# Turning the gated activations in an expert stage: three of four products with the identity become transposes

## What is computed

```python
a = jnp.einsum('nd,edf->nef', t, w_gate)
u = jnp.einsum('nd,edf->nef', t, w_up)
act = jax.nn.silu(a) * u * gate[..., None].astype(h.dtype)
out = jnp.einsum('nef,efd->nd', act, w_down)
```

## Time and profile before

| | us |
|---|---|
| median of 3 runs | 1609.87 |
| lowest and highest run | 1607.52, 1611.09 |
| the profiled execution | 1609.71 |
| its span, first to last instruction | 1608.0 |
| TensorE busy in the span | 1483.1 |
| DVE, ACT, POOL busy | 583.6, 175.2, 657.1 |

### The profile page before, as it was taken

The page is one execution under the profiler, slowest core; times in us unless marked ns, Lnnn a source line. Parts: engine busy times, 40 slices in busy tenths (PEclk is TensorE's granted clock), DMA queues, the critical chain, the costliest instruction groups (busy, mean ns, idle before and its releaser), DMA issues.

```text
span 1608.0 us, 24420 instructions
## 1 busy us (share of the span) xinstructions
PE 1483.1 (92%) x9906; PEld 1154.6 (72%) x9906; DVE 583.6 (36%) x1042; ACT 175.2 (11%) x281; POOL 657.1 (41%) x498
## 2 busy tenths in 40 slices
PE   5789999999959979999999899869999999999996
PEld 3789999998859969988777699754554454545534
DVE  3927668749561241112111621241212112212204
ACT  3000221000000000012222100121000000000002
POOL 4557697879947737753444557200000000000000
PEclk9889999999979989999999999979999999999998
DMA  7234444445534434463888434808999999999971
GB/s 236 79 118 145 130 158 131 157 157 186 174 104 147 153 105 150 146 259 128 325 327 330 146 132 157 340 1 354 397 422 399 396 423 397 379 423 397 400 311 59
DMA packets 106097, 376.99 MB, mean 234 GB/s; under 512 B 12405, under 2 KB 12405, under 8 KB 76274
## 3 DMA queue, kind: packets, MB, share of 16 engines
q1 hardware_dynamic: 103762, 371.68, 61.3%
q10 hardware_dynamic: 2272, 4.42, 0.8%
HBM read 369.30 MB, written 6.77 MB: 234 GB/s over the span
## 4 chain that ended last, share of the span: by engine, by line
PE 85%; DVE 11%; ACT 2%; issue 1%; DMA 1%; DVEq 0%; ACTq 0%; SPq 0%
PE ps L752 36%; PE ps L1048 14%; PE ps L799 11%; PE ps L1096 7%; PE ps L1110 4%; PE ps L1026 4%; PE ps L856 2%; DVE hT L1471 2%; DVE hT L1643 1%; PE ps L1065 1%; PE ps L874 1%; PE ps L864 1%; DVE hT L1420 1%; DMA A<-in_x_sample 1%; PE ps L695 1%
## 5 line engine op out<-in xcount | busy, mean ns | idle before, releaser
L752 PE MATMUL ps<-hT,tiles 128*128 128x144 f32 x2816 | 470.7, 291 | 49.3 <-ACT kv_stage L1234 16.8
L752 PEld LDWEIGHTS ps<-hT,tiles 128*128 128x128 f32 x2816 | 401.6, 194 | 52.8 <-issue 23.8
L652 POOL TENSOR_TENSOR tiles<-tiles 128x512 f32<-128x512 f32 x88 | 123.4, 1402 | 228.8 <-DMA tiles<-in_w_in 89.8
L1048 PE MATMUL ps<-tiles,A 128*64 128x512 f32 x576 | 171.2, 601 | 1.3 <-DVE A L1876 1.3
L752 PE MATMUL ps<-tiles 128*128 128x144 f32 x960 | 172.1, 289 | 0.0
L1441 DVE COPY pair_sums<-ps 128x144 f32<-128x144 f32 x44 | 13.5, 308 | 354.6 <-PE ps L752 354.6
L752 PEld LDWEIGHTS ps<-tiles 128*128 128x128 f32 x960 | 141.3, 193 | 0.0
L752 PE MATMUL ps<-A,tiles 128*128 128x144 f32 x768 | 138.2, 289 | 0.0
L799 PE MATMUL ps<-tiles,mT 128*128 128x256 f32 x512 | 133.3, 383 | 4.1 <-ACT kv_stage L1234 4.1
L655 POOL TENSOR_TENSOR tiles<-tiles 128x512 f32<-128x512 f32 x88 | 122.8, 1396 | 0.0
L657 POOL TENSOR_TENSOR tiles<-tiles 128x512 f32<-128x512 f32 x88 | 118.3, 1344 | 6.9
(11 more groups left out here) (287 smaller groups left out, 1741.6 us busy)
## 6 DMA issues: line engine op xcount, KB each, us to landing
tiles<-in_expert_w_down SPq DMA_DIRECT2D x56, 1024.0 KB, 10.0
tiles<-in_w_in SPq DMA_DIRECT2D x40, 1024.0 KB, 5.1
tiles<-in_expert_w_gate SPq DMA_DIRECT2D x40, 1024.0 KB, 11.3
A<-in_expert_w_up SPq DMA_DIRECT2D x32, 1024.0 KB, 9.4
tiles<-in_expert_w_up SPq DMA_DIRECT2D x32, 1024.0 KB, 12.6
tiles<-in_xa_w_k SPq DMA_DIRECT2D x16, 1024.0 KB, 5.1
tiles<-in_w_out SPq DMA_DIRECT2D x16, 1024.0 KB, 5.0
tiles<-in_xa_w_q SPq DMA_DIRECT2D x16, 1024.0 KB, 5.1
```

What stands on the lines that cost most here:

```text
L652: step.tick(tt(s1, a21, a22, ALU.add))
L752: return mm(one(u + mp, x, TH), w[:, kp, mp, :], rhs, start=(first and g == 0 and kp == 0), stop=(g == 3 and kp == 1), skip_group_check=True)
L1048: m = mm(ps[C * n:C * n + C, BRANCH_BANK, :], xe[:, b, C * s:C * s + C], moe_tile(t + 2 * g + n).rearrange("p (k n) -> p k n", k=KT)[:, k, :],
```

## The change

The four turns of `turn_act` were four matmuls with the identity. Now the first block is still such a matmul, and the other three are transposes with the same operands, the same identity and the same places in PSUM. The signal stays on the last one. `turn_act` is called twice a pair.

```diff
@@ -1062,8 +1062,11 @@
             def turn_act():
 
                 for k in range(KT):
-                    m = mm(ps[:, ACT_BANK, k * C:(k + 1) * C], act_nat[0:C, k * P:(k + 1) * P], ident[0:C, 0:C],
-                           start=True, stop=True)
+                    dst, own = ps[:, ACT_BANK, k * C:(k + 1) * C], act_nat[0:C, k * P:(k + 1) * P]
+                    if k == 0:
+                        mm(dst, own, ident[0:C, 0:C], start=True, stop=True)
+                    else:
+                        m = nc.tensor.transpose(dst, own, ident[0:C, 0:C])
                 m.then_inc(unit_done, 1)
```

## The result

| | before | after |
|---|---|---|
| median of 7 runs, us | 1607.79 | 1600.38 |
| lowest and highest, us | 1604.80, 1613.58 | 1593.77, 1601.44 |
| span of the profiled execution, us | 1608.0 | 1598.5 |

A forecast was written before the change was run, and what follows sets the result against it. TensorE was taken to bound the kernel. Turns of 0.52 us for 1.03 save 0.51 each, 16 x 0.51 = 8.1 us, bringing the median from 1609.87 to 1601.8 us; range 1599.2 to 1605.4.

The forecast's parts named there:

- The bound: Expert stage: TensorE sets the pace, the transfers have 2.6 us a pair in hand, so cuts in TensorE's stream shorten it.
- The passes: Each of 16 turns: three transposes replace six product passes, 0.52 us in place of 1.03, 8.1 us saved in all.
- the tail: End of a turn, from the last transpose's start to the next matmul group: 0.226 - 0.07 = 0.155 us.
- The head: Start of a turn: two product passes up to the first transpose, 2 x 0.118 = 0.236 us.
- The clock: Behind placing and turning, one fall to 1.2 GHz in one pair costs 1.7 us; not in the forecast's sum.
- the fall goes too: Rival: the shorter stretch of placing and turning avoids the one clock fall of 1.7 us, giving 1600.1 us; chance 0.12.
- The slower rival: Rival: transposes let the clock fall behind each pair's first turn, 5.5 us slower, 1615.4 us; chance 0.04.
- No gain: Rival: transposes take two passes each in the turns, or another wait takes the saving, 1609.9 us; chance 0.08.
- wide transposes: Rival: 64-row transposes or the step from product cost more; 5.9 us saved, 1604.0, or 3.5 and 1606.4; chance 0.16.

The follow-up runs named there:

- The padded second turn: Against the kernel before: second turn a product and three transposes, the last issued nine times; first turn keeps four products; ratio 0.9999.
- both turns padded: The changed kernel with each turn's last transpose issued nine times, so turns last as long as before; ratio to the kernel before 0.9981.
- the first padded: Against the kernel before: first turn a product and three transposes, the last issued nine times; second turn keeps four products; ratio 0.9979.

## Why the prediction was right in sign and short in size

*The bound.* Right. TensorE sets the pace: it is busy for 60.97 of 61.00 us in a pair, doubling the turns costs all of their length, and no transfer is among the releasers.

*The passes.* Right, and 0.4 us too high. Transposes are single passes of 0.063 us a step (forecast 0.066), and the tail is 0.15 us as forecast. The head was mis-sized: from the turn's start to the first transpose it is 0.27 us and not 0.24, since the mean step of 0.118 hides that the first step of a turn is longer. A turn costs 0.55 for the forecast's 0.52, and 0.48 is saved in place of 0.51: 7.7 us for 8.1.

*The clock.* This is the step that failed: the sum has no term for it. I had seen one fall in one trace and made "the fall goes too" a rival with a chance of 0.12 and a price of one fall, because the stretch gets shorter. The later traces of before show three falls and one in the loop, 5 in 21 pairs; the changed kernel has none in 21. And the reason, the shorter stretch, isn't the one that the runs bear out: padded to the old length, transposes still keep the clock. The mean granted clock gives an estimate of the size: 0.9620 over the 83 runs of before, 0.9641 over the 14 of the changed kernel. The time at 1.2 GHz is 2 x (1 - 0.9620) x 1607.9 = 122.2 us and 2 x (1 - 0.9641) x 1596.2 = 114.6; if all of it is work at half rate, half of the difference is lost time, 3.8 us (some 2 to 6 by the scatter of the runs). With the passes' 7.7 that is 11.5 of the 11.7 us between the mean spans. The falls seen in the loop are worth 5 x 1.7 / 3 = 2.8 us a run; where the remaining 1 us lies, if it is there at all, isn't shown. Passes and two falls, 8.1 + 3.4 = 11.5 us, would have come near the mean of the runs, but one trace with one fall couldn't give the second.

*The slower rival* was the wrong way round. The opening had shown that the clock rises while only transposes run; that the products taken out might themselves be what lets it fall I didn't ask. The Trainium skill, TensorE: Matmul & The Clock Gate, section Part 4: PE-mode transpose, says that transposes don't count as work for the full clock. For the fp32 transposes of this kernel the runs disagree: 1.00 through 64 transposes in six of seven pairs, 0.50 in and behind a stretch of products that was planned as long.

*No gain* and *wide transposes* didn't happen: 48 instructions, 0.063 us a step, and no extra step between product and transpose in the 64-row tile.

What stays open: with only the second turn changed the kernel gained 8.2 us (5.1 to 11.3) where 3.8 were due, and showed no fall in seven pairs, though its first turn is four products. At the 9 in 35 of the other such traces, seven pairs without a fall come by chance about one time in eight; but the five runs behind the ratio have a mean granted clock of 0.9644, as high as the changed kernel's, so luck in one trace is a poor explanation. The padded second turn, with pairs of the old length, has falls and the time of before; whether the shorter pair of 61.51 us matters wasn't tried by itself. The granted clock over the runs doesn't single out the first turn either: 0.9643 with both turns padded, but 0.9627 with only the first changed, 0.9626 with the first padded and 0.9616 with the second padded, each known to about 0.0007. So that the first turn's content counts rests on the times and on the falls in the loops. Nor is it settled what in a narrow product lets the clock fall.

## What to carry to other kernels

A turn by an fp32 product with the identity is two passes for a block, a transpose is one and shorter, 0.063 us for 0.112 here: where TensorE sets the pace, take the transpose. With the waits moved ahead of the matmul before it, a whole turn could be transposes here, 0.16 us a pair less again. Count the clock's falls over several executions before you price them: one trace shows one draw, and a fall in the trace of before is a term of the sum. Where a fall stands, look at what the engine did ahead of it, and ask which of these instructions the change takes away.

## What the runs showed of the hardware that I had not expected

Two stretches of about 4 us on TensorE, both without a gap and with the same operands, have opposite effects on its clock. 64 transposes of 64 x 128 leave it at 2.4 GHz in six of seven pairs, of 65.01 us; 36 passes of fp32 products of the same shape end at 1.2 GHz in every pair, 68.35 us, the granted clock 0.50 for 6.6 us. Even a turn of 1.03 us matters at equal length: with transposes in the first turn the kernel is 3.4 us (1.4 to 5.3) faster, with as long ones in the second it isn't (0.2 us, -1.9 to 2.1). The turn itself got no shorter, so the clock is the cause that suggests itself, but the granted clock of these runs doesn't confirm the whole amount.
